# Second and third attention: the probabilities are scaled by their inverse sums on GpSimd, between its weight slabs, in place of VectorE

## The reference, cut to what matters

```python
def windowed_gqa(h, w_qkv, w_o, sinks, cos, sin):       # second attention: 16 query heads of 64
    ...                                                 # q, k with rotary positions, bands of 3 x 128 keys
    s = jnp.where(mask[None, :, None, None], s, -jnp.inf)
    sink = sinks.astype(jnp.float32).reshape(1, 1, Hkv, G, 1, 1)
    m = jnp.maximum(jnp.max(s, axis=-1, keepdims=True), sink)
    e = jnp.exp(s - m)
    pr = e / (jnp.sum(e, axis=-1, keepdims=True) + jnp.exp(sink - m))
    o = jnp.einsum('bnhgqc,bnchd->bnqhgd', pr.astype(v.dtype), vb).reshape(B, S, Hq * d)
    return o @ w_o

def forgetting_attention(q, k, v, f_logit, b_forget, g_q, g_k):   # third attention: 8 heads of 64
    ...                                                 # q and k normalised by head, causal
    s = jnp.einsum("bhqd,bhkd->bhqk", qi, kh).astype(jnp.float32) * scale
    s = s + ci[..., :, None] - c[:, :, None, :]
    s = jnp.where(k_pos[None, :] <= q_pos[:, None], s, -jnp.inf)
    p = jax.nn.softmax(s, axis=-1).astype(vh.dtype)
    return jnp.einsum("bhqk,bhkd->bhqd", p, vh)
```

## Time and profile before

| | before |
|---|---|
| median of three runs | 2082.68 us (2082.54 to 2085.47) |
| profiled execution | 2086.29 us |
| its span | 2084.4 us |
| granted clock of TensorE, mean over the span | 0.992 |
| TensorE busy | 2052.5 us, 98% |
| VectorE busy | 1226.4 us, 59% |
| ScalarE busy | 941.9 us, 45% |
| GpSimd busy | 904.5 us, 43% |

### The profile page before, as it was taken

One profiled execution on the slowest core, in us unless ns is written; L12 is line 12 of the kernel. 1 busy time (PEld: TensorE's weight loads), 2 busy tenths in 40 slices (PEclk: granted clock), 3 DMA queues, 4 the chain that ended last, 5 costly groups with the idle time before them and its releaser, 6 DMA issues.

```text
span 2084.4 us, 28775 instructions
## 1 busy us (share of the span) xinstructions
PE 2052.5 (98%) x9998; PEld 1687.7 (81%) x9998; DVE 1226.4 (59%) x1842; ACT 941.9 (45%) x1495; POOL 904.5 (43%) x660
## 2 busy tenths in 40 slices
PE   9999999999999999899999999999999999999999
PEld 6778788888887878788888888878888788888887
DVE  7678757546265789856637266648879473213222
ACT  6455545434245566635424245535743544322222
POOL 5422235545455431044544456434214454455454
PEclk9999999999999999999999999999999999999999
DMA  4222122323223211022322323222103222232323
GB/s 166 91 72 75 51 74 98 111 91 101 92 101 111 81 62 39 24 91 81 104 99 101 98 94 112 91 86 87 42 21 111 81 91 94 88 111 91 101 92 111
DMA packets 52757, 183.22 MB, mean 88 GB/s; under 512 B 6576, under 2 KB 6832, under 8 KB 52656
## 3 DMA queue, kind: packets, MB, share of 16 engines
q1 hardware_dynamic: 51072, 177.76, 25.4%
q10 hardware_dynamic: 1584, 4.07, 0.5%
HBM read 176.04 MB, written 2.10 MB: 85 GB/s over the span
## 4 chain that ended last, share of the span: by engine, by line
PE 53%; issue 24%; POOL 14%; DVE 7%; ACT 2%; POOLq 0%; DVEq 0%; DMA 0%; ACTq 0%; SPq 0%
PE PS L545 52%; POOL wlo L537 14%; PE PS L777 1%; DVE AR L1931 1%; ACT AR L1203 1%; DVE AR L1934 0%; DVE ptlo L1821 0%; DVE acc L1646 0%; DVE AR L1813 0%; DVE AR L2295 0%; ACT AR L1339 0%; DVE nmax L1769 0%; DVE Blo L1951 0%; DVE AR L1947 0%; DVE Blo L2299 0%
## 5 line engine op out<-in xcount | busy, mean ns | idle before, releaser
L537 POOL TENSOR_TENSOR wlo<-raw,whi 128x512 fp32r<-128x512 f32 x656 | 904.2, 1401 | 1166.8 <-ACT whi L1106 1165.8
L545 PE MATMUL PS<-Bhi,whi 128*128 128x512 f32 x2352 | 926.7, 394 | 5.6 <-DVE AR L1732 2.7
L545 PE MATMUL PS<-Blo,whi 128*128 128x512 f32 x2352 | 916.7, 390 | 0.0
L545 PE MATMUL PS<-Bhi,wlo 128*128 128x512 f32 x2352 | 916.6, 390 | 0.0
L1106 ACT ACTIVATE whi<-raw 128x1024 fp32r<-128x1024 f32 x328 | 345.2, 1056 | 507.1 <-PE PS L545 431.3
L545 PEld LDWEIGHTS PS<-Bhi,whi 128*128 128x128 f32 x2352 | 442.1, 188 | 111.2 <-issue 14.6
L545 PEld LDWEIGHTS PS<-Bhi,wlo 128*128 128x128 f32 x2352 | 442.1, 188 | 92.8
L545 PEld LDWEIGHTS PS<-Blo,whi 128*128 128x128 f32 x2352 | 442.3, 188 | 90.0 <-issue 0.7
L1630 DVE TENSOR_TENSOR AR<-PS,R 128x512 f32<-128x512 f32 x170 | 115.3, 689 | 236.0 <-PE PS L545 224.2
L1686 DVE TENSOR_TENSOR X<-X,PS 128x512 f32<-128x512 f32 x88 | 60.3, 687 | 227.1 <-PE PS L545 226.4
L1931 DVE SCALAR_TENSOR_TENSOR AR<-AR,par_sb 128x511 f32<-128x511 f32 x88 | 116.9, 1329 | 8.8 <-ACT AR L1339 8.8
(11 more groups left out here) (240 smaller groups left out, 2091.7 us busy)
## 6 DMA issues: line engine op xcount, KB each, us to landing
raw<-in_weights SPq DMA_DIRECT2D x328, 512.0 KB, 3.2
AR<-AR SPq DMA_DIRECT2D x56, 64.0 KB, 2.0
X<-in_xT ACTq DMA_DIRECT2D x4, 512.0 KB, 7.1
out<-X SPq DMA_DIRECT2D x8, 256.0 KB, 3.5
AR<-in_pT ACTq DMA_DIRECT2D x2, 512.0 KB, 3.7
par_sb<-in_parameters ACTq DMA_DIRECT2D x1, 314.0 KB, 8.3
AR<-in_positions ACTq DMA_DIRECT2D x1, 256.0 KB, 8.2
con_sb<-in_constants ACTq DMA_DIRECT2D x1, 198.5 KB, 8.0
```

The lines of the kernel that those rows point to most:

```text
L537: ins = pool.tensor_tensor(wlo[:, j, c], raw[:, j % RAWS, c], f32(whi[:, j, c]), ALU.subtract)
L545: return pe.matmul(out, w, x, start=start, stop=stop)
```

## The change

In kinds 2 and 3 VectorE's `normalise` ends with the reciprocal, which raises a new semaphore, `rinv_ready`. The multiplications go to GpSimd: its stream, before a single loop of slabs, is written out for the two attentions. A scaling of two heads waits for `rinv_ready`, multiplies in place and raises `prob_ready` as before. GpSimd's slabs stand between the scalings, each behind the scaling of step g + 1, in the step g in which ScalarE makes the slab's copy. For the rest of the program the loop of slabs stays. Kind 1 is not changed.

```diff
+        rinv_ready = sem("rinv_ready")
...
+        RI0 = {2: 0, 3: 32}
...
         @block.gpsimd
         def _(pool):
-            with pool.Fori(0, SLABS // 4) as i:
-                for j in range(4):
-
-                    pool.wait_ge(hi_ready, 4 * i + j + 1)
-                    for c in (slice(0, D // 2), slice(D // 2, D)):
-                        ins = pool.tensor_tensor(wlo[:, j, c], raw[:, j % RAWS, c],
-                                                 f32(whi[:, j, c]), ALU.subtract)
-                    ins.then_inc(lo_ready, 1)
+            def low(s, slot):
+
+                pool.wait_ge(hi_ready, s + 1)
+                for c in (slice(0, D // 2), slice(D // 2, D)):
+                    ins = pool.tensor_tensor(wlo[:, slot, c], raw[:, slot % RAWS, c],
+                                             f32(whi[:, slot, c]), ALU.subtract)
+                ins.then_inc(lo_ready, 1)
+
+            def lows(first, end):
+                ...
+            def normalise(kind, g):
+
+                nb = band(kind, g % 4)[1]
+                c, b = (SC0[kind] + 2 * g) % 4, 2 * (g % 2)
+
+                pool.wait_ge(rinv_ready, RI0[kind] + g + 1)
+                for s in range(2):
+                    v = probs(kind)[:, b + s, 0:nb * P]
+                    pool.tensor_scalar(v, v, rinv[:, c + s:c + s + 1], None, ALU.mult).then_inc(prob_ready, 1)
+
+            begin = SLAB0["kq2"] + RING
+            lows(0, begin)
+            normalise(2, 0)
+            for g in range(4 * PAIRS[2]):
+                if g + 1 < 4 * PAIRS[2]:
+                    normalise(2, g + 1)
+                t = finished(2, g - 2)
+                if t is not None:
+                    low(begin + t, (begin + t) % RING)
+            after, begin = begin + NPROJ[2], SLAB0["qk3"] + 2 + RING
+            lows(after, begin)
+            normalise(3, 0)
+            for g in range(4 * PAIRS[3]):
+                if g + 1 < 4 * PAIRS[3]:
+                    normalise(3, g + 1)
+                t = finished(3, g)
+                if t is not None:
+                    low(begin + t - 4, (begin + t - 4) % RING)
+            lows(begin + NPROJ[3] - 4, SLABS)
...
                 else:
-                    own.step(dve.reciprocal(rinv[:, c:c + 2], rsum[:, c:c + 2]))
-                    own.wait()
-                    for s in range(2):
-                        v = pr[:, b + s, 0:nb * P]
-                        ts(v, v, rinv[:, c + s:c + s + 1], None, ALU.mult).then_inc(prob_ready, 1)
+                    dve.reciprocal(rinv[:, c:c + 2], rsum[:, c:c + 2]).then_inc(rinv_ready, 1)
```

More of the change, by code:

```diff
@@ new lines, in lows @@
+            def lows(first, end):
+                while first < end and first % 4:
+                    low(first, first % RING)
+                    first += 1
+                if end - first >= 4:
+                    with pool.Fori(first // 4, end // 4) as i:
+                        for j in range(4):
+                            low(4 * i + j, j)
+                    first = end // 4 * 4
+                for s in range(first, end):
+                    low(s, s % RING)
+            def normalise(kind, g):
[5 more added lines that the diff above has]
+                    pool.tensor_scalar(v, v, rinv[:, c + s:c + s + 1], None, ALU.mult).then_inc(prob_ready, 1)
```

## The result

Seven runs of the changed kernel have a median of 2091.26 us (2090.24 to 2092.34), seven of the kernel before 2085.47 us (2082.54 to 2087.19). The ratio is 1.0031 with a 95% interval of 1.0022 to 1.0041: **slower by 0.31%, 6.5 us**. The forecast was 2080.5 us, within a range up to 2088.0. Four single executions in the whole record, two of the kernel before and two of e8_act, stood far above the rest at a lower clock (2268 to 3388 us) and are in no ratio here.

The account below looks back on a forecast made before the run. TensorE, busy 2052.5 of 2084.4 us, was taken as the bound, leaving only its gaps and lower-clock time to gain. Middle 0, end -1.7, third -0.5 sum to -2.2 us: 2080.5 us, forecast's own range 2078.7 to 2082.5, whole range 2074.5 to 2088.

Parts of the forecast that it names:

- What GpSimd gets: Scalings moved to GpSimd: assumed 0.50, 0.76 and 1.00 us for 256, 384 and 512 columns, starting 0.22 us behind the reciprocal's start.
- from above: Upper side of GpSimd's scaling duration, from its two-input subtraction: 0.63, 0.95 and 1.27 us for 256, 384 and 512 columns.
- the estimate from that page of 0.58 us for 384 columns: GpSimd scaling duration by the Trainium skill, without a fixed part; it would make the sum some 0.5 us better.
- The slab stands behind one scaling pair, at most 1.7 us, and is read four tiles later: Second attention's middle: GpSimd's weight slabs between the scalings, delayed by a pair, were said to cost nothing new.
- Middle: 0.: Second attention, 775 to 850 us: TensorE asks for the probabilities late enough to hide the move, so no gain or loss.
- The deadline of 1.5 us behind the reciprocal: Second attention's middle, 256 columns: the second head's probabilities, at 1.22 + 0.1 us behind the reciprocal, fit under 1.5 us.
- End: -1.7 us.: Second attention, 850 to 885 us: freeing VectorE's queue wins 2.4 us in four steps, less 0.7 us for a slab.
- Third: -0.5 us.: Third attention, TensorE's waits between 1503 and 1521 us: net gain 0.5 us, bounds -1.3 to +0.8 us.
- The fear of this part, that a tap waits for a scaling: Third attention: a convolution tap reading two SBUF tensors waits for a GpSimd scaling it meets; +0.8 us if GpSimd always goes first.
- The wait of 2.35 us: Third attention, TensorE's gap at 1515.46 us: 0.67 to 0.8 us saved, one 0.76 us scaling between taps; net 0.
- GpSimd's scaling becomes the bound: Rival, chance 0.15: longer scalings make transposes wait, 7.2 us in the second attention's middle and 2 us in its end; 2091.9 us.
- The clock stays up: Rival, chance 0.23: gaps in both ends shrink, one lower-clock stretch goes, up to 5 us on top of the sum; 2075.5 us.

Follow-up runs that it names:

- e8_act: Kernel before, but in both attentions ScalarE scales the second head's probabilities while VectorE scales the first head's; ratio 1.0004 against the kernel before.
- e3_short: Changed kernel, but GpSimd scalings cover only the first 32, 88, 192 or 288 of 128, 256, 384 or 512 columns; ratio 0.9981 against the kernel before.
- e1: Changed kernel with only the second attention's scalings on GpSimd, the third's back on VectorE; ratio 1.0036 against the kernel before.
- e10: Changed kernel, but GpSimd scalings cover only 82, 172, 288 or 400 of 128, 256, 384 or 512 columns; ratio 1.0002 against the kernel before.
- e4: Kernel before, but probabilities of the second and third attention are scaled on no engine; ratio 0.9964 against the kernel before.
- e12: Kernel before with only the third attention's scalings on GpSimd, as a two-input multiplication with the factor repeated; ratio 0.9998 against the kernel before.
- e2: Changed kernel with only the third attention's scalings on GpSimd, the second's back on VectorE; ratio 1.0001 against the kernel before.

## Why the prediction was wrong

**The step that failed: "What GpSimd gets", its duration.** The prediction took four fifths of GpSimd's own subtraction, 0.50, 0.76 and 1.00 us, "since it is the same engine with one tensor less to read". Measured, least of each form: 0.60, 0.92, 1.24 and 1.56 us for 128, 256, 384 and 512 columns, 0.28 us and 2.5 ns a column. It is not only over the value taken but over the end "from above": the subtraction's 1.27 us for 512 columns with two inputs is no bound for an operation of another form. What the trace of before could not show was bounded from the nearest row as if fewer inputs meant less time. The sentences on the Trainium skill ("GPSIMD Engine Reference", section 4.1, one-input operations roughly at line rate, and section 3.1, at best about 1.8 cycles an element) leaned the same way: the estimate from that page of 0.58 us for 384 columns met 1.24, and the measurement decides. e3_short shows that this one term turned the sign: with the assumed durations the kernel gains 4.0 us, up to 2.5 of them by the clock.

**Start of the second attention.** The prediction had no term for it. It cost 1.9 us in the trace (1.1 in that of e1, which is the same there), by the slab of 757.52 behind a pair, and by pairs that are long. "The slab stands behind one scaling pair, at most 1.7 us, and is read four tiles later" looked at who reads the slab, not at VectorE's small operations that the later slab then meets.

**Middle: 0.** Measured +0.7 us with four waits of 0.41 us; 0 waits in e3 and e10. The deadline of 1.5 us behind the reciprocal was counted too early: in the step at 802.30 the second head's transposes would have started about 1.7 us behind it (1.29 + 0.44 of the first head's), so 0.72 us of scaling still fits. And a wait costs less than its length: 1.6 us of them made TensorE 0.7 us later, where the prediction had 0.1 us for 0.1 us.

**End: -1.7 us.** Measured +3.5, of which about 1.5 the clock's. With the assumed durations the whole second attention gave -2.7 in e3's trace, of which up to 1.7 are the clock's. So the direction was read rightly, but the size of what VectorE's queue is worth there, 1 us or a little more, is argued from single traces.

**Third: -0.5 us.** Measured -0.1. The fear of this part, that a tap waits for a scaling, came true in small only: three of the sixty taps met one and were held by 0.2 to 0.4 us (the last row below is one), and the mean tap went from 0.89 to 0.93 us. The long taps, up to 1785 ns before and 1780 after, are held by weight slabs. Mostly GpSimd waited, as in the first two rows:

```profile
1515.38 1.39 DVE L2205 SCALAR_TENSOR_TENSOR AR<-AR,par_sb 128x512 f32<-128x512 f32 x2
...
1515.56 3.46 POOL L563 TENSOR_SCALAR AR<-AR,rinv 128x384 f32<-128x384 f32 x2 [2.31 <-DVE rinv L1853]
...
1523.37 1.11 DVE L2205 SCALAR_TENSOR_TENSOR AR<-AR,par_sb 128x512 f32<-128x512 f32 x1
```

Two scalings of 384 columns take 2.48 us; here 3.46, the first of them 2.24. Two taps follow each other without a gap, and the first was begun 0.18 us before the scaling. By the rule of the Trainium skill's "SBUF — State Buffer" (section "Who interferes with whom": whichever starts first holds the shared pair for its whole instruction) the trace agrees for the first tap. The second was begun 0.47 us behind the scaling's start and took its usual 0.74 us, while the scaling was held by 1.0 us, more than the rest of the first tap (0.55 us); the rule alone doesn't say that. It is the moved work that pays in this place. The wait of 2.35 us became one of 1.75 and one of 0.67.

**The rivals.** "GpSimd's scaling becomes the bound" is what happened, given 0.15 and priced at +9.2 us; 6.5 were measured. Its pieces: 7.2 us for the middle were too many (0.7 measured, waits of 0.41 us in place of 0.8 each fourth step), 2 us for the end about right without the clock's share of the 3.5, and the start had no term. Its "against", the 1.27 us of the subtraction, was the same mistaken bound as in the forecast, so one error lay in both the value and its chance. "The clock stays up" came where the pair is gone altogether (e4: 1.00 in the third attention). Its reverse came as well: longer gaps put the clock at its lower level for 3 us more in the trace's end, and for 8 to 9 us more in the mean of the seven runs.

**The base.** The forecast started from 2082.68 us, the median of three runs; over more runs the kernel before lies at 2084.3 to 2085.5, in a spread of 2081 to 2088. 1.6 to 2.8 us of the distance between forecast and measured time are this.

What stays open: the clock's exact share of each ratio. The mean clocks bound it (at most 4.3 us of the 6.5), but its time at the lower level in an end differs between executions of the same instructions (7, 10 and 14 us between 850 and 900 us in before, e12 and e2), and no run held the clock up without adding work to TensorE.

## What to carry to other kernels

- The price of an operation on another engine can't be taken from a row of a different form on that engine, not even as an upper end: fewer inputs were slower here (0.92 us with a factor per row, 0.61 us with the factor as a repeated second tensor, 256 columns). Where no row has the form, keep the upper end well above the nearest row, and ask which form is the cheaper one.
- Unloading an engine that is full only pays up to the deadline of who reads the result: a pair of operations that moves to a slower engine reaches its second reader later by twice the difference of one. Work out the time from the producer to the first and to the last reader, step by step, and compare durations with that.
- Where TensorE's idle stretches let its clock fall, a change of 1 or 2 us in the waits can come out as 1 us or as 5: in the third attention waits shorter by 1.1 us went with a gain of 4.9 us in e4's trace, waits shorter by 1.6 us with 1.3 us in e12's. Traces say where the time goes; for the sign take many runs, and compare their mean clocks beside their times.

## What the runs showed of the hardware

GpSimd's multiplication of fp32 by a factor per row, in place: 0.60, 0.92, 1.24 and 1.56 us for 128, 256, 384 and 512 columns (2.5 ns a column and 0.28 us). The same as a tensor operation with the factor repeated by a step of zero: 0.40, 0.61, 0.83 and 1.04 us (1.7 ns a column and 0.18 us). The subtraction of two tensors: 1.26 us for 512. VectorE's factor per row: 0.35 and 0.42 us for 256 and 384. So here the factor as a repeated second tensor cost less than the same factor as a factor operand. It also cost less than the subtraction, but that is another operation with another output type, so the difference can't be put down to the input that stays at one address.
